# The differential attention stage: eight steps without a gate group instead of four, the last four groups behind the last row tile

## What is computed

```python
q = q.reshape(bsz, s, 2, D_HEADS, D_DH) * (D_DH ** -0.5)     # 2 components, 4 heads, 64 wide
sc = einsum('bqchd,bkchd->bchqk', qb, k) + alibi[None, None]
p = softmax(sc, axis=-1)
a = p[:, 0] - lam * p[:, 1]
o = einsum('bhqk,bkhv->bqhv', a, v)                          # v is 128 wide
y_d = rms_norm(o, subln_g) * (1.0 - lambda_init)
merged = g[0]*(y_a @ w_up_a) + g[1]*(y_b @ w_up_b) + g[2]*(y_c @ w_up_c) + g[3]*(y_d @ w_up_d)
```

## Time and profile before

| what | value |
|---|---|
| median of 3 runs | 2842.06 us (2841.2 to 2842.23) |
| the profiled execution | 2840.05 us, its span 2838.2 us |
| PE busy in the span | 2737.0 us |
| DVE busy, ACT busy | 1456.5 us, 1126.7 us |
| matmuls | 13218 |
| mean granted PE clock | 0.955 of full speed |

### The profile page before, as it was taken

The page is one execution under the profiler, slowest core; times in us unless marked ns, Lnnn a source line. Parts: engine busy times, 40 slices in busy tenths (PEclk is TensorE's granted clock), DMA queues, the critical chain, the costliest instruction groups (busy, mean ns, idle before and its releaser), DMA issues.

```text
span 2838.2 us, 33979 instructions
## 1 busy us (share of the span) xinstructions
PE 2737.0 (96%) x13218; PEld 2269.9 (80%) x13218; DVE 1456.5 (51%) x2736; ACT 1126.7 (40%) x1925; POOL 39.2 (1%) x62
## 2 busy tenths in 40 slices
PE   6999998999999999899999989999999999999997
PEld 5787776878888888778888877888888887788886
DVE  4644334765443555754444457554445477444444
ACT  4432223443364464633222244334536565322222
POOL 0000000000000010000000000000001000000000
PEclk9995559999999999999999999999999999999998
DMA  4320002322221342122333223123124321233322
GB/s 126 100 89 0 1 9 73 88 62 67 91 71 54 94 77 82 52 89 90 97 97 97 89 64 89 50 89 97 43 82 80 85 73 60 82 97 97 97 82 97
DMA packets 118430, 216.98 MB, mean 76 GB/s; under 512 B 14272, under 2 KB 21824, under 8 KB 118272
## 3 DMA queue, kind: packets, MB, share of 16 engines
q1 hardware_dynamic: 114528, 201.97, 23.4%
q0 software_dynamic: 3744, 12.85, 2.9%
HBM read 212.69 MB, written 2.10 MB: 76 GB/s over the span
## 4 chain that ended last, share of the span: by engine, by line
PE 36%; issue 18%; DVE 3%; ACT 1%; DMA 0%; POOL 0%; ACTq 0%; DVEq 0%; POOLq 0%
PE bank L526 17%; PE bank L529 12%; PE bank L626 2%; PE bank L615 1%; PE bank L591 1%; PE bank L592 1%; PE bank L558 1%; PE bank L655 1%; PE bank L672 1%; DVE wL L1323 0%; ACT wH L864 0%; DVE x L1800 0%; DVE gbuf L1900 0%; DVE sbufS L1875 0%; DVE sbufS L1877 0%
## 5 line engine op out<-in xcount | busy, mean ns | idle before, releaser
L1323 DVE TENSOR_TENSOR wL<-wraw,wH 128x1024 fp32r<-128x1024 f32 (+1 forms) x388 | 459.9, 1186 | 752.3 <-ACT wH L864 750.7
L864 ACT ACTIVATE wH<-wraw 128x1024 fp32r<-128x1024 f32 (+1 forms) x388 | 398.3, 1027 | 944.0 <-PE bank L526 509.7
L526 PE MATMUL bank<-wH,hH 128*128 128x512 f32 (+1 forms) x1248 | 495.4, 397 | 13.1 <-DVE wL L1323 3.7
L529 PE MATMUL bank<-hH,wH 128*128 128x512 f32 x1208 | 474.6, 393 | 7.3 <-DVE wL L1323 4.2
L526 PE MATMUL bank<-wH,hL 128*128 128x512 f32 (+1 forms) x1248 | 477.2, 382 | 0.0
L526 PE MATMUL bank<-wL,hH 128*128 128x512 f32 (+1 forms) x1248 | 476.9, 382 | 0.0
L529 PE MATMUL bank<-hH,wL 128*128 128x512 f32 x1208 | 471.5, 390 | 0.0
L529 PE MATMUL bank<-hL,wH 128*128 128x512 f32 x1208 | 471.3, 390 | 0.0
L526 PEld LDWEIGHTS bank<-wH,hH 128*128 128x128 f32 x1248 | 234.9, 188 | 67.2 <-issue 11.2
L526 PEld LDWEIGHTS bank<-wH,hL 128*128 128x128 f32 x1248 | 235.0, 188 | 49.0 <-issue 3.3
L529 PEld LDWEIGHTS bank<-hH,wH 128*128 128x128 f32 x1208 | 227.7, 188 | 56.3 <-DVE wL L1323 5.4
(11 more groups left out here) (301 smaller groups left out, 2970.4 us busy)
## 6 DMA issues: line engine op xcount, KB each, us to landing
wraw<-in_w_in_dram SPq DMA_DIRECT2D x180, 512.0 KB, 3.6
wraw<-in_w_ffn_down_dram SPq DMA_DIRECT2D x44, 512.0 KB, 3.4
wraw<-in_w_ffn_gate_dram SPq DMA_DIRECT2D x40, 512.0 KB, 3.6
wraw<-in_w_ffn_up_dram SPq DMA_DIRECT2D x40, 512.0 KB, 3.6
wraw<-in_w_out_dram SPq DMA_DIRECT2D x24, 512.0 KB, 3.5
tab<-in_rpb_rev_dram POOLq DMA_DIRECT2D x32, 224.0 KB, 6.3
wraw<-in_w_up_a_dram SPq DMA_DIRECT2D x8, 512.0 KB, 3.4
wraw<-in_w_up_b_dram SPq DMA_DIRECT2D x8, 512.0 KB, 3.5
```

Source lines behind the costliest of these rows:

```text
L526: mm = pe.matmul(bank[t][:, 0:b.cols], act_part[:, k, t * P:(t + 1) * P], w_part[:, kk, :], start=first, stop=last)
L529: mm = pe.matmul(bank[b.bank0 + t][:, :], w_part[:, kk, t * P:(t + 1) * P], act_part[:, k, :], start=first, stop=last)
L864: A(wH[:, u % W_SLOTS, 0:width], wraw[:, u % RAW_SLOTS, 0:width], ACT.Copy).then_inc(S["w_hi"], 1)
L1323: V.tensor_tensor(wL[:, u % W_SLOTS, 0:width], wraw[:, u % RAW_SLOTS, 0:width], wH[:, u % W_SLOTS, 0:width].bitcast(F32), ALU.subtract).th ...
```

## The change

Four more steps of the first component go without a group: 5, 7, 21 and 23. The number of groups stays 28, so the list is four longer (36 entries), and every group from the fourth of the list on stands later: after the change groups stand in steps 0, 2, 4, 6, 8 to 16, 18, 20, 22 and 24 to 35. The last four, the last unit of G31, stand in steps 32 to 35, behind the scores of item 31. PE, ACT and DVE read the same list; ACT's high parts of weight units move to steps 0, 8, 12, 16, 24, 28 and 32, DVE's low parts to 2, 9, 13, 18, 25, 29 and 33 (before 0, 6, 10, 14, 20, 24, 28 and 2, 7, 11, 15, 21, 25, 29), and the tanh evacuations of G30 from steps 10 to 13 to 12 to 15, those of G31 from 28 to 31 to 32 to 35.

```diff
-DIFF_IDLE = (1, 3, 17, 19)
+DIFF_IDLE = (1, 3, 5, 7, 17, 19, 21, 23)
```

## The result

The changed kernel took **2850.61 us** (median of 6 runs, 2847.31 to 2851.69), the kernel before 2841.35 beside it (6 runs, 2836.44 to 2842.23). The ratio is **1.0033**, with a 95% interval of 1.002 to 1.0046: +9.3 us, a third of a per cent slower, and clear of noise. The forecast was +12.4, with the time inside its range. The profiled run took 2847.31 us around a span of 2845.5; it is the fastest of the six.

What follows compares the result with a forecast made beforehand. PE, busy 96% of the span, was taken as the bound. Per layer 0 - 0.3 + 3.7 + 2 x 1.4 = 6.2 us, over two layers +12.4, median 2854.5 us; range 2845.5 to 2858.

Steps and rivals of the forecast that it cites:

- Part 1: Steps 5 and 7 lose their group: gain zero, since scores 8 wait for a row split; PE idles 2.6 us.
- The slip from 8 to 16: Possible delay from DVE's moved weight splits behind scores 8: estimated 0 to 0.15 us, taken as 0.
- Part 2: Steps 21 and 23 lose their group: 0.3 us gained per layer before scores 24, bounds 0 and 1.0.
- Part 3: Four groups in the tail, steps 32 to 35: scaling of the sums 3.7 us later per layer, bounds 2.22 and 5.44.
- Rival (c): Tail costs PE's share alone: +3.8 us without clock falls, 2845.9, or +9.4 with four; chance 0.10.
- Part 4: Clock falls behind the new gaps before scores 8 and 24: 1.4 us each, two per layer, bounds 0 and 1.7.
- rival (a): Clock stays high in the new gaps: +6.8 us, 2848.9; chance 0.28, counted for falls at none to two gaps.
- forecast case: Clock falls at three or four of the four new gaps; forecast +12.4 us, 2854.5; chance 0.55.
- Rival (b): Removed groups do shorten their steps, with row splits ready when PE is: -6.4 us, 2835.6; chance 0.05.

Runs made afterwards that it cites:

- first-pair experiment: Kernel before with only steps 5 and 7 also without a group, the last two groups in steps 32 and 33: 2842.98 us, ratio 1.0009.
- filled kernel: Changed kernel plus eight matmuls with unread results ahead of PE's wait for scores 8 and 24: 2846.19 us, ratio 1.0025.
- early row splits: Differential stage's row splits one step earlier: changed kernel 1.0055, kernel before 1.002, changed with squares ahead of last tanh 1.0045; only those for scores 8 and 24, changed kernel: 1.0014.
- the squares first: Changed kernel with ACT's tanh of the last group moved behind the squares of items 30 and 31: 2847.72 us, ratio 1.0023.
- the scaling first on the changed kernel: Changed kernel with DVE scaling the output of item s-4 ahead of the biased scores of item s in the differential stage: 2846.88 us, ratio 1.0026.
- scaling-first kernel: Kernel before with DVE scaling the output of item s-4 ahead of the biased scores of item s in the differential stage: 2836.3 us, ratio 0.9986.

## Why the prediction was right, and where it was off

**Part 1** (gain zero, 2.6 us of idle before scores 8): held. 11.90 against 11.91, idle 2.67 ended by L1430, and the first-pair experiment shows the same. Moving the chain by itself moved scores 8, by 0.95. The slip from 8 to 16, taken as 0, was a gain of 0.14 in the first layer; in the filled kernel it was -0.13 and +0.07.

**Part 2** (-0.3): 0.36 was measured. The idle before scores 24, forecast as 2.6 in one piece with 0.4 before scores 22, was 2.48 with 0.28. The cause that I named, ACT's and DVE's weight splits moving away from steps 20 and 21, fits the first-pair experiment, where they move and the groups at 21 and 23 stay, and the rows there show both parts of the sum: the exponential of step 20 came 0.60 later (0.7 forecast), that of 21 came 0.35 earlier (0.3). No run moved one split alone.

**Part 3** (+3.7): 2.22 for the products and 1.5 for the tanh and the squares; measured 2.21 or 2.22, and 1.50. The order on ACT was tested alone and gave 0.58, with the tanh still on the path for the rest. Rival (c), PE's share alone, is out: the distance grew by 3.7, not by 2.2. (The range was said to begin at (c) without falls, 2845.5; (c)'s own sum gives 2845.9.)

**Part 4** was mis-sized, and it is the one term of the sum that was. I took 1.4 us at each of four gaps, 5.6 in all. A fall costs about what I took: 1.30 in the first-pair experiment, 1.35 to 1.56 in the changed kernel, 1.6 with the early row splits. But not every gap brings one, and the granted clock of 0.5 that I expected behind each stood behind two of the four. I count 16 open gaps before scores 8 and 24 in four profiles: the changed kernel twice, the squares first, and the scaling first on the changed kernel. 8 of them brought a fall, 2 of 8 before scores 8 and 6 of 8 before scores 24. Half of four gaps at some 1.5 us are 3.0, and with 2 x 3.21 this makes +9.4.

The median moved by 9.3 in the first measurement, but by 6.9 when the same kernel was timed again, so the agreement with 9.4 is partly luck. By the number of falls the profiled run, with two, was rival (a)'s case, to which I gave 0.28; the forecast case, with three, is what the repeated profile showed. I had read "twice a fall behind 2.4 us" as a rule. Two cases bear a tendency at most: over all fourteen profiles those same two idles of 2.40 us brought a fall 18 times in 28.

**Rival (b)**, faster by 6.4, is out: its condition, the row splits ready when PE is, wasn't met. The earlier splits met it in part and only uncovered the next wait. The Trainium skill ("Perfetto Trace Analysis", section "Optimization Strategy") says that interleaving may help where the most-contended engine changes over time; here the trace does not bear it out, since the tail's idle was not free: groups there delayed the last product by 2.2 us and what follows it by another 1.5.

## What to carry to other kernels

Work taken out of steps where an engine is full shortens them only if nothing else ends there at the same moment; look at when the next operand would be ready if the engine had nothing to do, since a wait of length zero isn't on the list of waits. Work put into an idle tail is paid where it stands ahead of the tail's own work on its engine (2.2 us here), and again where another engine has to evacuate it in program order ahead of what ends the tail (1.5). And where removing work gains nothing, look for a loop of two in-order engines: changing the order within a step cost no operation here and gave the only gain over the kernel before.

## Unexpected of the hardware

The clock does not follow from the length of a gap alone. Behind the same idle of 2.67 us before scores 8 it fell in one layer and not in the other in three of the five profiles that have that gap, and stayed up in both layers in the other two. From 500 us on, all fourteen profiles together give this for idles of PE of 1.3 us and more in both layers:

| idle of PE, us | where | falls |
|---|---|---|
| 1.30 to 1.73 | several places | 0 of 38 |
| 1.92 to 2.00 | before scores 24, early row splits | 6 of 6 |
| 2.02 to 2.06 | before L615, early row splits | 3 of 6 |
| 2.40 | before L526, late in each layer | 18 of 28 |
| 2.44 to 2.48 | before scores 24 | 4 of 6 |
| 2.67 | before scores 8 | 3 of 10 |
| 2.86 | before scores 24, scaling first | 2 of 2 |
| 3.50 | before L558, in each layer | 21 of 28 |
| 3.44, 3.83, 4.02 | before the transposes behind the stage | 28 of 28 |
| 5.29 | before L558, first layer | 14 of 14 |

No idle up to 1.73 us brought a fall; from 1.92 to 3.50 it came and went. What tells the cases apart is open. Each low stretch inside the stage lasted 3.4 us.

A single profile can also hide a gain in a stage. The scaling-first kernel's span was 2838.5 against 2838.2 before, though its median is 4.7 us lower. Its two stages are 1.87 and 1.67 us shorter, but its first stage begins at 1117.70 against 1113.86, 3.84 us later, ahead of anything that the edit touches. So compare stages within a profile, and medians between kernels.
